# Two transformer blocks on one core: inverse roots by logarithm and exponential on ScalarE, fewer zero products, stick-breaking mixed with its projections, another order of expert rounds

## The reference

```
def rms_norm(x, g):   return x * lax.rsqrt(mean(x * x) + EPS) * g
def layer_norm(x, g, b):
    xc = x - x.mean(-1)
    return xc * lax.rsqrt(mean(xc * xc) + LN_EPS) * g + b

# first block: kind = MLA, stick-breaking, retention, MLA
for i in range(4):
    h = modulate(rms_norm(x, norm_g[i, 0]), sh_a, sc_a)
    x = x + g_a * rms_norm(mixer(h), norm_g[i, 1])
    h = modulate(rms_norm(x, norm_g[i, 2]), sh_f, sc_f)
    x = x + g_f * rms_norm(square(relu(h @ w1)) @ w2, norm_g[i, 3])

# stick-breaking, 16 heads of 64
z = (q @ k.T) * scale
log_1m = where(strict, log_sigmoid(-z), 0)
suffix = reverse_cumsum(log_1m) - log_1m
a = where(strict, exp(log_sigmoid(z) + suffix), 0);  y = (a @ v) @ w_out

# retention: o = o * rsqrt(mean(o*o) + EPS) * gn_g;  y = (silu(g) * o) @ w_out

# second block, 2 layers: x = layer_norm(ALPHA * x + mixer(h)), x = layer_norm(ALPHA * x + moe(h))
# layer 0: Fourier mixing beside grouped attention with rms-normed, rotated q and k
# layer 1: neighbourhood attention
# moe: 64 experts, 8 for each token:  y += w * ((silu(x @ w_gate) * (x @ w_up)) @ w_down)
```

## Time and profile before

| | us |
|---|---|
| median of 3 runs | 3436.77 |
| the profiled execution | 3431.49 |
| its span on the core | 3429.8 |
| TensorE busy | 3214.2 (94%) |
| TensorE in the chain that ended last | 75% |
| DMA in that chain | 11% |
| VectorE in that chain | 7% |
| TensorE waiting for ring pieces at L1406 | 74.0 |
| VectorE busy | 1361.6 (40%) |
| ScalarE busy | 518.1 (15%) |

### The profile page before, as it was taken

The page is one execution under the profiler, slowest core; times in us unless marked ns, Lnnn a source line. Parts: engine busy times, 40 slices in busy tenths (PEclk is TensorE's granted clock), DMA queues, the critical chain, the costliest instruction groups (busy, mean ns, idle before and its releaser), DMA issues.

```text
span 3429.8 us, 39837 instructions
## 1 busy us (share of the span) xinstructions
PE 3214.2 (94%) x14378; PEld 2172.7 (63%) x14378; DVE 1361.6 (40%) x3066; ACT 518.1 (15%) x1086; POOL 402.2 (12%) x462
## 2 busy tenths in 40 slices
PE   7999989999999999999999999999999999899897
PEld 4888877888888887888755434444435676333333
DVE  4766525566023566476463422222213033111112
ACT  2300112001011002200022311111111022111011
POOL 0000111000010000000220222222113001010000
PEclk9999999999999999999999999999999999999999
DMA  7688633774435774367310599999995215999995
GB/s 299 242 326 300 244 111 139 295 288 173 159 111 196 294 281 148 124 257 256 137 37 1 228 360 379 360 391 369 359 349 191 86 38 222 412 412 409 411 407 241
DMA packets 135315, 860.80 MB, mean 251 GB/s; under 512 B 20576, under 2 KB 24032, under 8 KB 37600
## 3 DMA queue, kind: packets, MB, share of 16 engines
q1 hardware_dynamic: 94128, 665.89, 49.6%
q0 software_dynamic: 40288, 191.41, 16.3%
q10 hardware_dynamic: 720, 1.13, 0.1%
HBM read 846.28 MB, written 35.13 MB: 257 GB/s over the span
## 4 chain that ended last, share of the span: by engine, by line
PE 75%; DMA 11%; DVE 7%; issue 4%; ACT 1%; SPq 1%; POOL 0%; POOLq 0%; DVEq 0%; ACTq 0%
PE ps L769 14%; PE ps L1119 13%; PE ps L1406 11%; PE ps L1100 9%; DMA ring<-stream_in 9%; PE ps L866 8%; PE ps L1430 6%; PE ps L1448 2%; PE ps L1367 2%; DMA arena<-mod_stream_in 2%; DVE arena L1934 2%; PE ps L781 1%; PE ps L824 1%; PE ps L833 1%; PE ps L1221 1%
## 5 line engine op out<-in xcount | busy, mean ns | idle before, releaser
L1406 PE MATMUL ps<-ring,arena 128*64 128x512 f32 (+2 forms) x2112 | 565.3, 637 | 75.7 <-DMA ring<-stream_in 74.0
L1934 DVE SCALAR_TENSOR_TENSOR arena<-arena,cond 128x512 f32<-128x512 f32 x602 | 426.6, 748 | 91.7 <-DMA arena<-mod_stream_in 82.6
L1119 PE MATMUL ps<-arena,ring 128*128 128x256 f32 x2048 | 445.1, 379 | 4.5 <-DVE arena L2248 4.5
L1406 PEld LDWEIGHTS ps<-ring,arena 128*64 128x64 f32 (+2 forms) x2112 | 201.1, 152 | 385.2 <-issue 380.1
L1119 PEld LDWEIGHTS ps<-arena,ring 128*128 128x128 f32 x2048 | 387.9, 190 | 57.5 <-issue 5.5
L1100 PE MATMUL ps<-H,ring 128*128 128x256 f32 x1920 | 420.0, 379 | 0.2
L1100 PEld LDWEIGHTS ps<-H,ring 128*128 128x128 f32 x1920 | 362.3, 190 | 49.6 <-issue 1.7
L1430 PE MATMUL ps<-ring,arena 128*64 128x512 f32 (+2 forms) x1056 | 288.4, 612 | 20.9 <-issue 13.2
L1598 ACT ACTIVATE arena<-ps 128x512 f32<-128x512 f32 (+2 forms) x331 | 167.6, 506 | 749.8 <-PE ps L769 305.5
L2457 DVE TENSOR_TENSOR arena<-arena,ps 128x256 f32<-128x256 f32 x76 | 32.0, 421 | 584.7 <-ACT arena L1822 584.6
L1430 PEld LDWEIGHTS ps<-ring,arena 128*64 128x64 f32 (+2 forms) x1056 | 95.5, 146 | 186.0 <-issue 171.2
(11 more groups left out here) (286 smaller groups left out, 3255.7 us busy)
## 6 DMA issues: line engine op xcount, KB each, us to landing
ring<-stream_in SPq DMA_DIRECT2D x612, 1024.0 KB
arena<-mod_stream_in POOLq DMA_DIRECT2D x130, 1024.0 KB, 5.1
arena<-mod_stream_in SPq DMA_DIRECT2D x8, 1024.0 KB, 13.5
YS<-mod_stream_in SPq DMA_DIRECT2D x6, 1024.0 KB, 5.1
moe_out<-zeros POOLq DMA_DIRECT2D x18, 256.0 KB, 7.7
arena<-stream_in SPq DMA_DIRECT2D x4, 1024.0 KB, 5.9
stat<-stream_in SPq DMA_DIRECT2D x2, 1024.0 KB, 4.7
moe_in<-YS POOLq DMA_DIRECT2D x1, 2048.0 KB, 7.6
```

The costliest lines, as they stand in the source:

```text
L1119: m = mm(out[:, i * T:(i + 1) * T], w[:, c * P:(c + 1) * P], f_h[:, 16 * half + c, :], start=(half == c == 0), stop=(half == 1 and c == 15))
L1406: m = mm(out[at, :], e_xt[:, k % 2, 4 * part + c, at], w[:, c * TC:(c + 1) * TC], start=(part == c == 0), stop=(part == 1 and c == 3))
L1934: ins = stt(acc, w, x, acc, MUL, ADD)
```

## The change

1. `inverse_root`: ScalarE reads the mean of squares from PSUM with Ln, and then takes Exp of minus half of it in place. VectorE's reciprocals go; it waits for the drained bank alone. `log_exp_tables` loads the table set that holds both functions ahead of the first pre-norm, every post-norm and every layer norm. In retention and in grouped attention nothing calls it; the head norms of grouped attention get four buffers in place of two.
2. `keep_warm` after an RMS norm issues 12 instructions in place of 14; after the layer norms 16, 16 and 10 in place of 36, 36 and 22.
3. Stick-breaking starts its iterations after q0, k0 and q1; the other nine projections stand between the sums and the values of iterations 0 to 6. The output product's first parts are begun in iterations 8 and 9. The masks come by a half-megabyte load on ScalarE's queue into `YS` instead of a ring piece, so every later piece moves up by one place.
4. The 28 expert rounds of layer 1 get another order; their number by kind stays (8 S, 12 P, 8 Q).

```diff
+SB_ORDER = ["q0", "k0", "q1", "k1", "v0", "q2", "k2", "v1", "q3", "k3", "v2", "v3"]
+SB_BESIDE = {0: ["k1"], 1: ["v0"], 2: ["q2"], 3: ["k2", "v1"], 4: ["q3"], 5: ["k3", "v2"], 6: ["v3"]}
...
-            order["sb_in", l] = Phase([0, 1, 2, 3, 4, 5, 6, 7, 0, 1, 2, 3], 13)
+            order["sb_in", l] = Phase([0, 1] + [6, 7] * 5, 12)
...
-    second = in_turn("SPQSPPQ" * 4, {"S": 0, "P": 8, "Q": EXPERTS - 32})
+    second = in_turn("QSPPQSPQSPPQSPPPPSQSQPSQSPPQ", {"S": 0, "P": 8, "Q": EXPERTS - 32})
...
+        s_const, s_const_full = YS[:, 0:1024], mod_first_full[3]
...
-            def keep_warm(b, count=7):
+            def keep_warm(b, count=6):
...
             def stick(l):
...
-                for k in range(1, 8):
-                    pair(ph, k, k, h_lat, waits=wait_h(2 * l) if k == 1 else None)
-                for k in range(4):
-                    token_major(ph, 8 + k, 8 + k, (0, 1))
-                w, used = take(ph, 12)
-                tri, ones = w[:, 0:P], w[:, P:2 * P]
...
+                projected("k0")
+                projected("q1")
                 for i in range(SB_H // 2 + 2):
                     both(i, logits)
                     both(i - 1, sums)
+                    for name in SB_BESIDE.get(i, ()):
+                        projected(name)
                     both(i - 2, values)
+                    if i >= SB_H // 2:
+                        out_begun(i - SB_H // 2, i - 3)
+                for k in range(2):
+                    out_ended(k, k + 5)
...
-                    keep_warm(5, (18, 18, 11)[m])
+                    keep_warm(5, (8, 8, 5)[m])
...
+            def log_exp_tables():
+                act.preload_act_table_set("natural_log_exp_and_others")
+
+            def inverse_root(ph, k, out, in_, **kw):
+
+                b = wait_filled(act, ph, k)
+                link(fn(out, in_(ps[:, b, :]), ACT.Ln, bias=eps, **kw))
+                fn(out, out, ACT.Exp, scale=-0.5).then_inc(drained[b], 1)
...
-                drain(PLAN["norm", 2 * s + 1], 0, STD[:, 0:T], left, ACT.Sqrt, bias=eps)
+                inverse_root(PLAN["norm", 2 * s + 1], 0, RSTD[:, 0:T], left)
...
                 def deviation(h):
-                    drain(ph, 12 + h, stat[:, h, 0:T], left, ACT.Sqrt, scale=D / float(RET_V), bias=eps)
+                    inverse_root(ph, 12 + h, stat[:, h, T:TC], left, scale=D / float(RET_V))
...
                         if c >= 4:
                             act.wait_ge(ab_normed, c - 3)
                         inverse_root(ph, 12 + c, stat[:, c % 4, :], whole, scale=D / float(P))
...
-            def reciprocal_deviation(n):
+            def wait_deviation(n):
                 wait_drained(dve, PLAN["norm", n], 0)
-                link(v.reciprocal(RSTD[:, 0:T], STD[:, 0:T]))
...
+                act.dma_start(s_const, stream[SB_CONST][:, 0:1024]).then_inc(s_const_full, 16)
```

More of the change, by code:

```diff
@@ L1026, in values, with out_begun, out_ended @@
                         m.then_inc(filled[b], 1)
+                def out_begun(k, n):
+                    w, used = take(mix, k)
+                    out, _ = bank(mix, k)
+                    for c in range(n):
+                        wait_drained(pe, ph, 5 * c + 4)
+                        m = mm(out[:, 0:T], w[:, c * 256:c * 256 + P], s_o[:, c, :], start=(c == 0), stop=False)
+                        if c == k == 0:
+                            m.then_inc(used, 1)
+                def out_ended(k, n):
+                    w, (b, _) = slot(mix, k), mix.fill(k)
+                    for i in range(2):
+                        for c in range(0 if i else n, 8):
+                            if not i:
+                                wait_drained(pe, ph, 5 * c + 4)
+                            m = mm(ps[:, b, i * T:(i + 1) * T], w[:, c * 256 + i * P:c * 256 + (i + 1) * P], s_o[:, c, :],
+                                   start=(i == 1 and c == 0), stop=(c == 7))
+                            if k and i == 0 and c == n:
+                                m.then_inc(piece_used[mix.piece(k - 1)[0]], 1)
+                    m.then_inc(filled[b], 1)
+                projected("k0")
+                projected("q1")
                 for i in range(SB_H // 2 + 2):
@@ L1030, in stick @@
                     both(i - 1, sums)
+                    for name in SB_BESIDE.get(i, ()):
+                        projected(name)
                     both(i - 2, values)
-                mixed, ph = ph, PLAN["mix_out", l]
-                for k in range(4):
-                    pair(ph, k, k, [s_o[:, c, :] for c in range(8)], waits=None if k else lambda c: wait_drained(pe, mixed, 5 * c + 4))
+                    if i >= SB_H // 2:
+                        out_begun(i - SB_H // 2, i - 3)
+                for k in range(2):
+                    out_ended(k, k + 5)
+                for k in range(2, 4):
+                    pair(mix, k, k, [s_o[:, c, :] for c in range(8)])
             def retention(l):
@@ L1618, in pre_norm @@
                         fn(SQ[:, c, :], X[:, c, 0:T], ACT.Square).then_inc(sq_act, 1)
-                drain(PLAN["norm", 2 * s], 0, STD[:, 0:T], left, ACT.Sqrt, bias=eps)
+                inverse_root(PLAN["norm", 2 * s], 0, RSTD[:, 0:T], left)
                 for c in range(DC):
@@ L1702, in stick @@
                     both(i, logs)
+                    for name in SB_BESIDE.get(i, ()):
+                        if name[0] != "k":
+                            projected(name)
             def sines(w):
@@ L2164, in stick, with projected @@
             def stick(l):
-                ph = PLAN["sb_in", l]
-                first_halves(2 * l, ph, [s_q[:, c, :] for c in range(2)])
-                for k in range(4, 8):
-                    drain(ph, k, s_k[:, 2 * (k - 4):2 * (k - 4) + 2, :], pairs)
+                into = PLAN["sb_in", l]
+                first_halves(2 * l, into, [s_q[:, c, :] for c in range(2)])
+                def projected(name):
+                    j = int(name[1])
+                    drain(into, SB_ORDER.index(name), s_k[:, 2 * j:2 * j + 2, :], pairs)
+                projected("k0")
                 ph = PLAN["sb", l]
@@ L3020, in pieces_of @@
         elif l % 3 == 1:
-            yield from by_columns(inp["sb_w_in"][j], 256)
-            yield con["sb"]
+            parts = dict(zip([n + str(i) for n in "qkv" for i in range(4)], by_columns(inp["sb_w_in"][j], 256)))
+            yield from (parts[name] for name in SB_ORDER)
             yield from by_columns(inp["sb_w_out"][j], 256)
@@ L3072 @@
     con = shape_constants()
-    stream = np.zeros((PIECES + SHARED_PIECES, P, PIECE), np.float32)
+    stream = np.zeros((SB_CONST + 1, P, PIECE), np.float32)
     n = 0
```

79 lines of the change are left out of this document (47 added, 32 removed).

## The result

The changed kernel takes 3379.73 us (median of 3 runs, 3377.58 to 3381.49); its ratio to the kernel before is 0.9832, 95% interval 0.9809 to 0.9854. Two later sets of runs on other chips gave 0.9857 (0.9842 to 0.9872) and 0.9855 (0.9842 to 0.9869), 49.1 and 50.6 us less than the kernel before took beside them (medians 3432.12 and 3431.63). The profiled execution took 3377.58 with a span of 3375.9, 53.9 less than that of before; forecast were 45.2 less.

What follows compares the result with a forecast made beforehand. TensorE, busy 94% of the span, was taken as the bound, so other engines' changes count only by its waits. Terms summed to 45.2 us off 3431.49, 3386.3, plus 5.3 for the median: 3391.6, range 3375 to 3408.

Steps and rivals of the forecast that it cites:

- Post-norms: Norm after a mixer or FFN: root to scaling 1.02 us instead of 2.36, saving 1.34 each, 9.4 for seven.
- signs of being wrong: Projections waiting for their banks, clock falling where zeros were taken away, or DMA share in expert rounds below 0.95.
- MLA: MLA's query norm, two of them: TensorE's wait of 2.31 us shortened by 1.3 each, 2.6 saved.
- Retention: Four head norms: eight table loads where there was one, 2 us lost, bounds 1 to 4.
- Last FFN: Modulation work there: 0 forecast; only two zero products behind the last FFN go, 0.5 us.
- Grouped attention and layer norms: Grouped attention's first rotation 3.2 us earlier plus 1.8 of clock, 5.0 saved; four layer norms together 9.0.
- Stick-breaking: Nine projections fill TensorE's waits: 19.1 us of waits and half clock, 2.4 remaining, 16.7 saved; bounds 10 to 18.
- Expert rounds: Layer 1: a round of four first restarts the ring's loads sooner, 4 us saved; bounds 0 and 22.
- Dear switches: Rival: each of retention's eight table loads costs twice its 1.28 us row, 10.2 more, 3401.8; chance 0.07.
- Half the overlap: Rival: stick-breaking's overlap is half what it looks, 8 us less, experts' 4 gone too, 3403.6; chance 0.20.
- full loads: Rival: the experts' order gives 22 us of idle loading in place of 4, 3373.6; chance 0.11.
- The one-expert rounds: Slower rival: one-expert rounds stop layer 1's loads, 8.5 us each, 68 over all eight, 3463.6; chance 0.03.

## Why the prediction was right, and where its terms were off

The chains that the forecast shortened were the right ones, and the time of 3391.6 was 12 above the measured 3379.73 (8.7 by the profiled executions). That is inside the range of 3375 to 3408, but below the 3383 to 3400 that the bounds of its own terms gave. Against the kernel before in the same set, 45.2 less stand against 57.0, 49.1 and 50.6 less, so part of the distance lies in how slow the kernel before was in the first set (3436.77, and 3431.63 to 3432.60 in the later ones). The largest terms that the sum lacked are the clock in MLA and in retention (1.7 each) and the last FFN (2.4); and that stick-breaking came so near is in part luck, as told below.

**Post-norms.** Right to 0.01 us each, and the idle time left (0.39 for 0.38) shows that the zeros don't bind. The clock didn't fall behind the norms where zeros were taken away, which was one of the signs of being wrong. The pre-norms gained nothing, as said: the second half of the first pair covers them.

**MLA.** The step was right (2.31 of waiting became 0.97), the term too small. What was left out is the clock: in layer 0 the 24 products behind the wait had run partly at 1.2 GHz, 1.7 us. In layer 3 the same wait of 2.30 in the old kernel left them at 5.45, so this part isn't earned everywhere (in the run with fewer zeros alone the clock fell there too, and layer 3's mixer took 1.7 longer).

**Retention.** The delay came as computed: VectorE's last scaling, 1014.30 before and 988.12 now, is 1.6 later against its surroundings (which had gained 27.8 by then). But TensorE ended level. The term was -2 and measured 0.1: TensorE's waits from norm to norm rose from 2.4 to 4.0, near the 2 forecast, though most of it is a new wait of 1.40 for ScalarE's square and not the wait for GpSimd; and 1.7 of half clock is gone. The old kernel's clock falls behind its wait of 1.62, and the new kernel's, with four shorter waits (0.50, 0.49, 1.06, 0.49), does not. Windows of before, then of the changed kernel:

```profile
1016.00:1020.00 4.00, 2.76 (x8) 2.04 (x9) 0.98 (x1) 0.00 (x0) 1.96 (x2) 0.81 0.00 0
1020.00:1024.00 4.00, 4.00 (x15) 3.33 (x15) 0.00 (x0) 0.00 (x0) 0.00 (x0) 0.77 0.30 98
```

```profile
988.00:992.00 4.00, 2.44 (x9) 1.36 (x8) 2.99 (x4) 1.36 (x2) 2.88 (x3) 1.00 0.00 0
992.00:996.00 4.00, 3.51 (x17) 3.12 (x17) 0.00 (x0) 0.00 (x0) 0.44 (x1) 1.00 0.25 33
```

I had put the clock on the wrong side, as a risk of the new kernel. Of the six traces with the old root five show the fall behind retention (0.57 to 0.81), of the eight with the new root none. The sixth, that of the zero products in MLA's wait, has the same wait of 1.62 and no fall, and this layer's mixer takes 254.3 us there where it takes 256.0 before: that prices the half clock at 1.7, with this layer's program unchanged, and it shows that the wait alone doesn't settle the clock. No run filled this wait by itself, so that its length has a part in it is argued from MLA's case, not shown here.

```profile
1016.00:1020.00 4.00, 2.46 (x10) 1.88 (x11) 1.28 (x1) 0.00 (x0) 2.26 (x2) 1.00 0.00 0
1020.00:1024.00 4.00, 4.00 (x21) 3.52 (x20) 0.00 (x0) 0.00 (x0) 0.00 (x0) 1.00 0.59 211
```

**Last FFN.** Forecast 0, measured 2.4. VectorE's modulation work, which TensorE waits for, came late three times (0.17, 1.42, 1.46) and now once (1.38). The likely cause is that reciprocals off the chain still took VectorE's time, which was needed a little later; no run isolates it. These waits add up to 2.6 to 4.3 in the six traces with the old root, and to 1.3 to 2.8 in the seven with the new root and zero products.

**Grouped attention and layer norms.** The rotation came 3.2 earlier, as forecast, and the clock gave 2.3 where 1.8 was taken. The layer norms' own 9.0 were 9.2 on ScalarE and VectorE. The 1.9 lost at the expert layers' heads is not a price of the roots. In layer 0 the gather of the first expert's rows landed 1.1 later, but this head takes 41.1 to 43.9 over all traces, whatever the kernel (41.1 in another trace of the changed one); and the 0.8 in layer 1 belongs to the order of the rounds. At layer norm 1 the clock fell.

**Stick-breaking.** The waits left are the forecast two. Against 16.7 stand 17.8: TensorE's idle time from norm to norm went from 15.7 to 2.7, which is 13.0, and its busy time fell by 4.8. By the granted clock 0.8 of this is half clock (2.3 lost at the start before, 1.5 lost at the end now); the same products also take 4.0 less where no wait stands between them. The forecast had all this in one sum, 51.3 less 32.2 of steady work, so its gain came out near although it took the projections at half their length. The size is a draw too: the stretch takes 169.3 to 171.3 us in the traces with the old order of work and 150.0 to 151.9 in those with the new, for what the clock does. The sums behind the last wait, in this trace, where the clock fell, and in the next one of the same kernel, where it didn't:

```profile
506.34 1.62 PE L1025 MATMUL ps<-arena,YS 128*128 128x384 f32 x2 [1.29 <-POOL arena L2766]
```

```profile
506.51 0.88 PE L1025 MATMUL ps<-arena,YS 128*128 128x384 f32 x2 [1.29 <-POOL arena L2766]
```

**Expert rounds.** Forecast 4; 7.2 in the first pair of traces, 3.2 as a mean of thirteen, less the 0.8 ahead of them.

**The rivals.** Dear switches are refuted: 1.28 each, with 0.02 and 0.01 on either side. By the rule of the Trainium skill (*ScalarE: Activation LUTs*, "What ACT_TABLE_LOAD costs") each switch would have cost another 1.38; the trace doesn't agree here, neither behind independent nor behind dependent work (0.02 us between the end of that work and the load). Half the overlap is refuted by the windows, full loads by the 519.3 us mean. The one-expert rounds didn't stop the loads: the share over all of them is 1.00 (0.99 before):

```profile
2845.00:3335.00 490.00, 441.07 (x2084) 169.46 (x2084) 82.42 (x282) 52.72 (x108) 33.33 (x34) 0.95 1.00 408
```

Clock is the term that the forecast handled worst. Reading the traces in stretches of 4 us and summing busy time times what the clock lacks of 1, the old kernel shows 41.9 us of such loss and the changed one 28.3. This sum counts places where TensorE waits for loads anyway, so it is a bound and not a price, and it is a draw as well (35.4 and 27.5 in two more traces of the changed kernel); but 1.7, 2.3 and 1.7 of it were earned at the three places above, MLA, grouped attention and retention.

## What to carry to other kernels

A chain of small steps on engines beside TensorE is priced best by its start-to-start times, instruction by instruction: this came out to hundredths. Then ask how long TensorE stood still before, and what its clock did behind that: removing 1.3 us of a 2.3 us wait gave 3 us where the clock had fallen. Filler products belong to the length of the gap, so look at both together: fewer of them on the old gaps cost 4 us, and none at all on the new ones 12.3; whether fewer help on the shorter gaps no run could tell.

## What the runs showed of the hardware

- The same idle time of TensorE was followed by half clock in some places and executions and not in others. 2.3 us in MLA: by a fall in layer 0 in five of five traces, in layer 3 in one of five. 2.9 us behind RMS norms without zeros: five of seven. 1.62 us in retention: five of six. 1.42 and 1.29 close together at the end of stick-breaking: five of eight, and there the first sums behind them take 1.62 in place of 0.88. Waits of 0.5 to 1.1 with products between them (retention, six traces) were not followed by a fall.
- That draw moves an unchanged stretch by up to 2 us between executions (169.3 to 171.3 for old stick-breaking), and a whole layer of experts differs by up to 5 (723.2 to 728.2 for the same kernel). Of a change in one stretch, a single pair of traces tells the mechanism, not the size.
- A table load between Ln and Exp that depend on each other takes 1.28 us, with 0.02 ahead of it and 0.01 behind; without a load 0.03 lie between the two.
- Exp on 128x256 from SBUF took 0.42 us and on 128x512 0.63.
